# A hybrid mLSTM and latent attention step: two tiles' statistics ahead of the sample skip on VectorE, two inverse roots ahead of the gate product on GpSimd

## The chip, the cores and the metric

The kernel runs on one core of a Trainium2 chip. Its time is the device time of one execution in microseconds; the median of 3 runs is given. All arithmetic is float32. A core has a matrix engine (TensorE, PE in the profile), three engines for elementwise work (VectorE = DVE, ScalarE = ACT, GpSimd = POOL), an engine that here issues all transfers (SyncE = SP, its DMA queue SPq), and 16 DMA engines.

## What is computed

A prompt of 512 frames and 8 streams of 16 new frames (the sample rows) go through one mLSTM layer and one attention layer that share their weights. The change is in the mLSTM layer, which has 4 heads of width 512. Cut to what matters:

```
for each head:
    s   = (q k^T) * w_intra                       # within a chunk, causal
    num = w_inter * (C q) + s v
    den = w_inter * (n q) + sum(s)
    h   = num / max(|den|, exp(-m))
    C_new = decay * C + (v * w_upd)^T k           # 8 old states of 512 x 512 per head, and one new one
    n_new = decay * n + sum(w_upd * k)
hn = (h - mean(h)) * rsqrt(var(h) + eps) * outnorm_w     # per row and head
y  = (hn + skip * xc) * silu(z)
x  = x + y @ w_out
```

Then follow the shared latent keys and values, the attention layer and the output norms, which the change doesn't touch.

## The kernel before

The 640 rows are 5 tiles of 128: tiles 0 to 3 are the prompt, tile 4 (`NP`) holds the sample rows. Each engine has its own program, written out by hand in order, and the programs are tied by semaphores. No scheduler moves anything. An engine that waits holds up all that stands behind it in its program.

The four heads (numbered 0 to 3) run from about 310 to 570 us. In each, TensorE runs eight steps (`step(h, n)`: the products with one eighth of the old states, L1001, and their updates, L1016) mixed with the values of the prompt tiles (`prompt_values`, L1025), the transposition of normalised tiles (`turn`, L1034), and four quarters of the prompt's new state (`prompt_c`, L1049); then it starts the projections of the next head (`project_head`: L887, L900) and its scores.

A prompt tile goes round the engines like this: TensorE writes its values into PSUM and raises `pv_mm`; VectorE's `statistics(h, t)` (L2154 to L2173, seven small operations) raises `var_ready`; GpSimd's `inverse_root(h, t)` (L2617 to L2621) raises `pow_ready`; ScalarE's `normalise(h, t)` (L1611) empties the PSUM bank and raises `norm_done`; TensorE turns the tile. `prompt_c(h, 0)` writes into the bank of tile 2, so it waits for `norm_done` of that tile.

The sample rows of head h - 1 are finished in head h: VectorE adds the skip (`add_skip(h - 1, ...)`, L2201, four operations of 128x128; it raises `y_added`), and GpSimd multiplies by the gate (`gated(h - 1, ...)`, L2638; it waits for `y_added` and raises `y_ready`). GpSimd's `add_k(h, t)` (L2632) sums the weighted keys of the prompt tiles.

SyncE issues all transfers on one queue in a written order. Per step: the store of the updated state (L617, 1 MB) once VectorE's `update` (L2181) is done, then the load of a later state (L569, 1 MB) once the store of the step before has landed. Behind step 1 stands the load of the gate rows into `zh` (L624, 1.25 MB):

```
if n == 1:
    if h:
        sp.wait_ge(y_ready, 2 * h)
    sp.dma_start(zh, chunks(z_dram, h, slice(0, T))).then_inc(hz_in, 16)
```

The count 2h is reached by `gated(h - 1, slice(SEQ, T), 2)`, the last reader of the old `zh`. The load of the rows m (L602) comes next. The four quarters of the prompt's new state are copied out of PSUM by ScalarE's `keep_c(h, q)` (L1629, raises `pc_out`) into two buffers in turn, and stored (L592, 256 KB each: quarter 0 before step 4's store, 1 and 2 before step 5's, 3 before step 6's). So the copy of quarter 3 waits until the store of quarter 1 has landed:

```
if 2 * h + q // 2:
    act.wait_ge(cp_out[q % 2], 16 * (2 * h + q // 2))
```

`project_head(h + 1)` waits for `pc_out` of all four quarters of head h, and so does `first_out` (L720), the output projection behind head 3.

Of the kernel before, what the change touches and what calls it, by code (L numbers as in the profile page):

```python
# [155 lines left out]
def program(nc, i, o):  # L156

    with ExitStack() as ctx:
# [1666 lines left out]
        def _(dve):  # L1825
# [319 lines left out]
            def keep_sums(h):  # L2145
                dve.wait_ge(small_mm, 2 * h + 1)
                v.tensor_copy(den_s, small[:, 0:16]).then_inc(small_out, 1)
                dve.wait_ge(small_out, 2 * h + 1)

            def statistics(h, t):  # L2150
                src = pair_bank[t % 2] if t < NP else stream_h
                own, den = tiny[:, t], den_s[:, S_DEN + t:S_DEN + t + 1]
                dve.wait_ge(pv_mm, TT * h + t + 1)
                v.bn_stats(st6[:, t], src).then_inc(dve_own, c.up(dve_own))  # L2154
                if t == NP:
                    v.tensor_tensor(nqm, den_s[:, S_NQ:S_NQ + STREAMS], wq_mask[:, h], ALU.mult).then_inc(dve_own, c.up(dve_own))
                    dve.wait_ge(dve_own, c.all(dve_own))
                    v.reduce_sum(nq[:, 0:1], nqm, AX_X).then_inc(dve_own, c.up(dve_own))
                    dve.wait_ge(dve_own, c.all(dve_own))
                    v.tensor_tensor(nq[:, 1:2], nq[:, 0:1], den, ALU.add).then_inc(dve_own, c.up(dve_own))  # L2160
                    dve.wait_ge(dve_own, c.all(dve_own))
                    den = nq[:, 1:2]
                v.scalar_tensor_tensor(own[:, 1:2], den, -1.0, den, ALU.mult, ALU.max).then_inc(dve_own, c.up(dve_own))
                dve.wait_ge(dve_own, c.all(dve_own))
                v.bn_aggr(mv[:, t], st6[:, t]).then_inc(dve_own, c.up(dve_own))
                v.tensor_tensor(own[:, 1:2], own[:, 1:2], cols[:, 1, t, h:h + 1], ALU.max).then_inc(dve_own, c.up(dve_own))
                dve.wait_ge(dve_own, c.all(dve_own))
                v.reciprocal(own[:, 2:3], own[:, 1:2]).then_inc(dve_own, c.up(dve_own))
                dve.wait_ge(dve_own, c.all(dve_own))
                op = v.tensor_scalar(own[:, 4:5], mv[:, t, 1:2], own[:, 2:3], None, ALU.mult)  # L2170
                op.then_inc(dve_own, c.up(dve_own))
                dve.wait_ge(dve_own, c.all(dve_own))
                op = v.tensor_scalar(own[:, 3:4], own[:, 4:5], own[:, 2:3], EPS, ALU.mult, ALU.add)  # L2173
                op.then_inc(var_ready, 1)

            def update(h, n):
                s, par = STEPS * h + n, n // KH
                for g in range(4):
                    b = 2 * g + par
                    dve.wait_ge(upd_mm, 4 * s + g + 1)  # L2180
                    op = v.scalar_tensor_tensor(ct[s % CS][:, g, :], ct[s % CS][:, g, :], decb[:, h, b:b + 1],  # L2181
                                                bank[g][:, :], ALU.mult, ALU.add)
                    op.then_inc(upd_done, 1)
# [12 lines left out]
            def add_skip(h, part, tile):  # L2196
                dve.wait_ge(turn_out, TT * h + tile + 1)
                for q in range(KH):
                    n = h * KH + q
                    raised = y_added if q == KH - 1 else dve_own  # L2200
                    v.scalar_tensor_tensor(h_t[:, q, part], xc[:, n, part], vec[:, V_SK + n:V_SK + n + 1],  # L2201
                                           h_t[:, q, part], ALU.mult, ALU.add).then_inc(raised, c.up(raised))
# [14 lines left out]
            for h in range(HEADS):  # L2217
                keep_sums(h)
                statistics(h, 0)
                update(h, 0)  # L2220
                statistics(h, 1)
                update(h, 1)
                if h:
                    add_skip(h - 1, slice(SEQ, T), NP)
                statistics(h, 2)
                statistics(h, 3)
                update(h, 2)
                update(h, 3)
                update(h, 4)
                update(h, 5)  # L2230
                add_skip(h, slice(0, SEQ), NP - 1)
                new_n(h)
                update(h, 6)
                if h + 1 < HEADS:
                    head_front(h + 1)
                update(h, 7)
                if h + 1 < HEADS:
                    weighted_scores(h + 1, 0)
                statistics(h, NP)
                if h + 1 < HEADS:  # L2240
                    weighted_scores(h + 1, 1)
                    stream_queries(h + 1)
                    for t in range(2, TT):
                        weighted_scores(h + 1, t)
# [263 lines left out]
        def _(pool):  # L2508
# [105 lines left out]
            def inverse_root(h, t):  # L2614
                own = tiny[:, t]
                pool.wait_ge(var_ready, TT * h + t + 1)
                g.tensor_tensor(own[:, 4:5], own[:, 3:4], half_neg, ALU.pow).then_inc(pool_own, c.up(pool_own))  # L2617
                pool.wait_ge(pool_own, c.all(pool_own))
                g.tensor_tensor(own[:, 5:6], own[:, 4:5], own[:, 2:3], ALU.mult).then_inc(pool_own, c.up(pool_own))
                pool.wait_ge(pool_own, c.all(pool_own))  # L2620
                op = g.tensor_scalar(own[:, 6:7], mv[:, t, 0:1], own[:, 5:6], -1.0, ALU.mult, ALU.mult)  # L2621
                op.then_inc(pow_ready, 1)

            def add_k(h, t):
                if t == 1:
                    pool.wait_ge(kw_ready, 6 * (h + 1))
                    first = kh[:, :, 0, :]
                else:
                    pool.wait_ge(pool_own, c.all(pool_own))
                    first = kwsum  # L2630
                raised = kwsum_ready if t == NP - 1 else pool_own
                g.tensor_tensor(kwsum, first, kh[:, :, t, :], ALU.add).then_inc(raised, c.up(raised))  # L2632
# [21 lines left out]
            for h in range(HEADS):  # L2654
                sum_weights(h)
                inverse_root(h, 0)
                inverse_root(h, 1)
                if h:
                    gated(h - 1, slice(SEQ, T), 2)
                add_k(h, 1)  # L2660
                inverse_root(h, 2)
                add_k(h, 2)
                inverse_root(h, 3)
                add_k(h, 3)
                if h + 1 < HEADS:
                    head_basis(h + 1)
                gated(h, slice(0, SEQ), 1)
                inverse_root(h, NP)
# [241 lines left out]
```

## Time and profile before

| | us |
|---|---|
| median of 3 runs | 1042.89 (1042.45 to 1043.36) |
| the profiled execution's own time | 1039.92 |
| its span | 1038.1 |
| TensorE busy | 1010.7 |
| VectorE busy | 520.0 |
| GpSimd busy | 300.6 |
| ScalarE busy | 258.0 |

The granted clock of TensorE is full in all of the 40 slices. Busy time of an engine adds up its instructions; what is worth something to the time is where TensorE stands idle, and who ends that. A row of a timeline merges instructions of a kind that follow each other; in brackets stand the idle time before them and the instruction that ended it.

### The profile page before, as it was taken

The page shows a single profiled execution, that of the slowest core. Times are in us where ns is not written, and L with a number is a line of the kernel's source. Part 1 is how long each engine was busy: PE and PEld are TensorE (multiplying, and loading weights), DVE is VectorE, ACT ScalarE, POOL GpSimd, SP SyncE. Part 2 cuts the span into 40 slices and gives each one's busy share as a digit, 9 for nine tenths or more (in the row PEclk, how much of TensorE's full clock was granted, in tenths as well). Part 3 has the DMA queues.
Part 4 walks back from the last instruction along what each step waited for, and adds up shares of the span by engine and source line. Part 5 has one row for each costly group of instructions (what it writes and reads, how often), then busy time and mean ns, then how long its engine had stood idle before and what let it go on. Part 6 is the DMA issues. An engine that isn't in the chain of part 4 may idle for free.

```text
span 1038.1 us, 12026 instructions
## 1 busy us (share of the span) xinstructions
PE 1010.7 (97%) x4310; PEld 648.1 (62%) x4310; DVE 520.0 (50%) x1149; ACT 258.0 (25%) x541; POOL 300.6 (29%) x361
## 2 busy tenths in 40 slices
PE   7999999999989999999999999999999999999998
PEld 5777777777754453443535677777766666656655
DVE  6955444444466566685665522334244444344224
ACT  3212121212154242232421000011213323243221
POOL 3652525252313234142232053411440303010110
PEclk9999999999999999999999999999999999999999
DMA  7324232423275988979799432022210201213202
GB/s 271 98 80 158 97 113 105 157 91 111 112 286 191 399 329 345 370 303 392 300 350 340 154 107 71 32 81 104 93 63 1 84 17 68 73 47 128 79 27 102
DMA packets 44465, 164.21 MB, mean 158 GB/s; under 512 B 4916, under 2 KB 8248, under 8 KB 35456
## 3 DMA queue, kind: packets, MB, share of 16 engines
q1 hardware_dynamic: 44416, 163.56, 42.8%
q8 instruction: 30, 0.49, 0.2%
q14 instruction: 19, 0.16, 0.0%
HBM read 106.32 MB, written 57.23 MB: 158 GB/s over the span
## 4 chain that ended last, share of the span: by engine, by line
PE 85%; DVE 8%; ACT 2%; POOL 2%; DMA 1%; issue 1%; SPq 0%; DVEq 0%; POOLq 0%; ACTq 0%
PE work_a L825 11%; PE work_b L825 9%; PE work_a L720 7%; PE work_b L720 5%; PE work_b L1258 5%; PE work_a L1049 5%; PE bank L1133 5%; PE work_b L1342 4%; PE work_a L948 4%; PE bank L770 3%; PE bank L1016 2%; PE work_b L1133 2%; PE work_b L1001 2%; DVE arena L2181 2%; PE work_a L1328 2%; PE bank L1303 2%
## 5 line engine op out<-in xcount | busy, mean ns | idle before, releaser
L2181 DVE SCALAR_TENSOR_TENSOR arena<-arena,bank 128x512 f32<-128x512 f32 x128 | 87.1, 743 | 58.7 <-PE bank L1016 58.7
L1049 PE MATMUL work_a<-arena 128*128 128x512 f32 x128 | 64.1, 613 | 2.8 <-ACT arena L1611 2.8
L825 PE MATMUL work_a<-arena 128*128 128x320 f32 x224 | 64.9, 433 | 0.4 <-DVE arena L1948 0.4
L825 PE MATMUL work_a<-arena,ring 128*128 128x320 f32 x224 | 64.9, 432 | 0.0
L825 PE MATMUL work_b<-arena 128*128 128x320 f32 x224 | 62.8, 432 | 0.0
L720 PE MATMUL work_a<-arena,ring 128*128 128x320 f32 x192 | 54.2, 441 | 6.8 <-DMA ring<-in_stream 6.8
L825 PEld LDWEIGHTS work_b<-arena 128*128 128x128 f32 x224 | 42.6, 190 | 17.7
L720 PE MATMUL work_b<-arena,ring 128*128 128x320 f32 x192 | 52.8, 432 | 0.0
L2716 POOL COPY arena<-arena 32x640 f32<-32x640 f32 x20 | 16.9, 844 | 123.1 <-ACT arena L1726 116.9
L825 PEld LDWEIGHTS work_a<-arena 128*128 128x128 f32 x224 | 41.5, 190 | 16.1 <-issue 0.6
L825 PEld LDWEIGHTS work_a<-arena,ring 128*128 128x128 f32 x224 | 41.5, 190 | 15.5
L720 PEld LDWEIGHTS work_a<-arena,ring 128*128 128x128 f32 x192 | 37.2, 195 | 22.2 <-DMA ring<-in_stream 6.8
L2638 POOL TENSOR_TENSOR xc<-arena 128x2048 f32<-128x2048 f32 (+1 forms) x8 | 23.2, 2897 | 89.4 <-DVE arena L2201 89.4
L1493 ACT ACTIVATE arena<-arena 128x128 f32<-128x128 f32 x16 | 5.0, 314 | 168.0 <-DVE arena L1908 150.5
L770 PEld LDWEIGHTS bank<-arena 128*128 128x128 f32 x320 | 41.6, 190 | 7.0 <-ACT arena L1519 2.1
L720 PEld LDWEIGHTS work_b<-arena,ring 128*128 128x128 f32 x192 | 36.4, 190 | 15.0
L770 PE MATMUL bank<-arena 128*128 (+1 forms) x320 | 42.6, 280 | 1.1 <-ACT arena L1519 1.1
L1973 DVE SCALAR_TENSOR_TENSOR arena<-arena,vec 128x512 f32<-128x512 f32 x48 | 38.1, 795 | 5.0 <-ACT arena L1500 1.6
L948 PE MATMUL work_a<-xc,arena 128*128 128x128 f32 (+3 forms) x136 | 39.2, 431 | 0.7 <-ACT arena L1546 0.7
L1025 PE MATMUL work_a<-arena 128*128 128x512 f32 x80 | 38.1, 607 | 0.0
L1049 PEld LDWEIGHTS work_a<-arena 128*128 128x128 f32 x128 | 21.1, 190 | 26.5 <-issue 26.5
L1016 PE MATMUL bank<-arena 32*128 32x512 f32 x256 | 36.5, 640 | 0.0
(349 smaller groups left out, 1917.4 us busy)
## 6 DMA issues: line engine op xcount, KB each, us to landing
ring<-in_stream SPq DMA_DIRECT2D x66, 512.0 KB, 3.7
arena<-in_c SPq DMA_DIRECT2D x32, 1024.0 KB, 9.2
out_s_c<-arena SPq DMA_DIRECT2D x32, 1024.0 KB, 6.6
arena<-in_keys SPq DMA_DIRECT2D x8, 664.0 KB, 4.1
v_scratch<-arena SPq DMA_DIRECT2D x16, 320.0 KB, 4.4
k_scratch<-arena SPq DMA_DIRECT2D x16, 320.0 KB, 4.7
z_scratch<-arena SPq DMA_DIRECT2D x16, 320.0 KB, 4.2
arena<-k_scratch SPq DMA_DIRECT2D x4, 1280.0 KB, 12.6
```

Of the source, the lines that this page charges most:

```text
L720: done = mm(halves(buf)[:, a, :], lhs, rhs[:, a * HALF:(a + 1) * HALF], start=first, stop=last)
L770: last = mm(bank[2 * q + t // 3][:, at:at + VG], lhs, basis[:, q, n, :], start=True, stop=True)
L825: last = mm(quarter[q], weights[:, k, :], tokens_of[:, k, :], start=fresh and k == 0, stop=k == KH - 1, skip_group_check=True)
L948: last = mm(score_bank(h, t), k_t[:, q, q0:q0 + P], xc[:, h * KH + q, q0:q0 + WID[t]], start=q == 0, stop=q == KH - 1)
L1016: mm(bank[g][:, :], kz[h % 2][rows, par, q, :], v_s[h % 2][rows], start=True, stop=True, tile_position=(32 * g, 0)).then_inc(upd_mm, 1)
L1025: last = mm(pair_bank[t % 2], weights_of(s, t), vh[:, :, s, :], start=s == 0, stop=s == t)
L1049: last = mm(pair_bank[q % 2], kh[:, q, t, :], vh[:, :, t, :], start=t == 0, stop=t == NP - 1)
L1133: last = mm(dst[:, 0:HALF], weights[:, k, :], tokens_of[:, k, :], start=k == 0, stop=k == KD - 1)
L1258: last = mm(work[1][:, w * SEQ:(w + 1) * SEQ], out_weight(t, k), og[:, k, 0:SEQ], start=k == 0, stop=k == KD - 1)
L1342: last = mm(dst, weights[:, k, :], tokens_of[:, k, :], start=fresh and k == 0, stop=k == KH - 1, skip_group_check=True)
L1973: op = v.scalar_tensor_tensor(a0, xin[s][:, tap:tap + SEQ], w, a0, ALU.mult, ALU.add)
L2181: op = v.scalar_tensor_tensor(ct[s % CS][:, g, :], ct[s % CS][:, g, :], decb[:, h, b:b + 1], bank[g][:, :], ALU.mult, ALU.add)
```

## The change

In VectorE's program `statistics(h, 2)` and `statistics(h, 3)` go ahead of the skip of the preceding head's sample rows. In GpSimd's program `inverse_root(h, 2)` and `inverse_root(h, 3)` and two of the three `add_k` go ahead of the gate product of those rows, and `inverse_root(h, 3)` ahead of `add_k(h, 2)`.

```
@@ VectorE
                 update(h, 0)
                 statistics(h, 1)
                 update(h, 1)
+                statistics(h, 2)
+                statistics(h, 3)
                 if h:
                     add_skip(h - 1, slice(SEQ, T), NP)
-                statistics(h, 2)
-                statistics(h, 3)
                 update(h, 2)
@@ GpSimd
                 sum_weights(h)
                 inverse_root(h, 0)
                 inverse_root(h, 1)
+                add_k(h, 1)
+                inverse_root(h, 2)
+                inverse_root(h, 3)
+                add_k(h, 2)
                 if h:
                     gated(h - 1, slice(SEQ, T), 2)
-                add_k(h, 1)
-                inverse_root(h, 2)
-                add_k(h, 2)
-                inverse_root(h, 3)
                 add_k(h, 3)
```

VectorE's program in head 1, from the update of step 1 to that of step 2, before. L2154 opens one tile's statistics and L2173 closes them, L2201 is the skip, `work_a` the PSUM banks of the tiles.

```order
L2181 SCALAR_TENSOR_TENSOR arena<-arena,bank 128x512 x4
L2201 SCALAR_TENSOR_TENSOR arena<-xc,vec,arena 128x128 x4
L2154 BN_STATS arena<-work_a 128x6
L2163 SCALAR_TENSOR_TENSOR arena<-arena 128x1
L2165 BN_AGGR arena<-arena 128x2
L2166 TENSOR_TENSOR arena<-arena 128x1
L2168 RECIPROCAL arena<-arena 128x1
L2170 TENSOR_SCALAR arena<-arena 128x1
L2173 TENSOR_SCALAR arena<-arena 128x1
```

The same place now, from the opening of tile 3's statistics on (those of tile 2 stand ahead of it).

```order
L2154 BN_STATS arena<-work_a 128x6
L2163 SCALAR_TENSOR_TENSOR arena<-arena 128x1
L2165 BN_AGGR arena<-arena 128x2
L2166 TENSOR_TENSOR arena<-arena 128x1
L2168 RECIPROCAL arena<-arena 128x1
L2170 TENSOR_SCALAR arena<-arena 128x1
L2173 TENSOR_SCALAR arena<-arena 128x1
L2201 SCALAR_TENSOR_TENSOR arena<-xc,vec,arena 128x128 x4
L2181 SCALAR_TENSOR_TENSOR arena<-arena,bank 128x512 x16
```

The skip stands behind both tiles' statistics, and the four updates that follow stand directly behind the skip.

GpSimd's program at the same place, before: from the gate product (L2638) to the last `add_k` (L2632); L2617 opens an inverse root.

```order
L2638 TENSOR_TENSOR xc<-arena 128x4x128
L2632 TENSOR_TENSOR arena<-arena 128x512
L2617 TENSOR_TENSOR arena<-arena 128x1
L2619 TENSOR_TENSOR arena<-arena 128x1
L2621 TENSOR_SCALAR arena<-arena 128x1
L2632 TENSOR_TENSOR arena<-arena 128x512
L2617 TENSOR_TENSOR arena<-arena 128x1
L2619 TENSOR_TENSOR arena<-arena 128x1
L2621 TENSOR_SCALAR arena<-arena 128x1
L2632 TENSOR_TENSOR arena<-arena 128x512
```

And now.

```order
L2632 TENSOR_TENSOR arena<-arena 128x512
L2617 TENSOR_TENSOR arena<-arena 128x1
L2619 TENSOR_TENSOR arena<-arena 128x1
L2621 TENSOR_SCALAR arena<-arena 128x1
L2617 TENSOR_TENSOR arena<-arena 128x1
L2619 TENSOR_TENSOR arena<-arena 128x1
L2621 TENSOR_SCALAR arena<-arena 128x1
L2632 TENSOR_TENSOR arena<-arena 128x512
L2638 TENSOR_TENSOR xc<-arena 128x4x128
L2632 TENSOR_TENSOR arena<-arena 128x512
```

The gate product has gone behind two `add_k` and both inverse roots. The programs of TensorE, ScalarE and SyncE are the same as before.

## Rows read from the trace of the kernel before

**Rows 1.** The page, parts 1 and 2 (GB/s moved in 40 slices).
```profile
PE 1010.7 (97%) x4310; PEld 648.1 (62%) x4310; DVE 520.0 (50%) x1149; ACT 258.0 (25%) x541; POOL 300.6 (29%) x361
GB/s 271 98 80 158 97 113 105 157 91 111 112 286 191 399 329 345 370 303 392 300 350 340 154 107 71 32 81 104 93 63 1 84 17 68 73 47 128 79 27 102
```

**Rows 2.** Waits of TensorE and SyncE, 310 to 570: us, times, longest.
```profile
PE work_a L887 <- issue: 3.1, 3, 1.6
PE work_a L1049 <- ACT arena L1611: 2.8, 3, 0.9
SPq L624 <- POOL xc L2638: 4.6, 3, 1.5
```

**Rows 3.** Timeline of TensorE: start, us, line, operation, [idle before <- releaser].
```profile
365.48 1.13 PE L887 MATMUL work_a<-xc,arena 128*128 128x128 f32 x8 [1.28 <-issue]
...
395.97 3.60 PE L1025 MATMUL work_a<-arena 128*128 128x512 f32 x8
...
402.55 1.95 PE L1049 MATMUL work_a<-arena 128*128 128x512 f32 x4 [0.92 <-ACT arena L1611]
...
428.69 1.13 PE L887 MATMUL work_a<-xc,arena 128*128 128x128 f32 x8 [0.31 <-issue]
```

**Rows 4.** Timeline of ScalarE, end of heads 1 and 3.
```profile
428.00 0.60 ACT L1629 ACTIVATE arena<-work_a 128x512 f32<-128x512 f32 x1 [6.34 <-DMA out_p_c<-arena]
...
555.67 0.60 ACT L1629 ACTIVATE arena<-work_a 128x512 f32<-128x512 f32 x1 [6.34 <-DMA out_p_c<-arena]
```

**Rows 5.** Busy time in a stretch of head 1, clock, DMA share, GB/s.
```profile
393.00:428.00 35.00, 34.08 (x158) 14.03 (x158) 22.46 (x47) 8.49 (x23) 12.24 (x22) 1.00 1.01 383
```

**Rows 6.** Single issues (first and last start) and their time to landing.
```profile
L617 SPq DMA_DIRECT2D out_s_c<-arena x1: 343/343/343, 391.7 to 391.7; - x1
DMA to landing us min/median/max: 4.8/4.8/4.8
...
L592 SPq DMA_DIRECT2D out_p_c<-arena x1: 901/901/901, 418.5 to 418.5; - x1
DMA to landing us min/median/max: 9.4/9.4/9.4
...
L592 SPq DMA_DIRECT2D out_p_c<-arena x1: 332/332/332, 556.3 to 556.3; - x1
DMA to landing us min/median/max: 2.8/2.8/2.8
```

**Rows 7.** Timeline of VectorE, head 1.
```profile
386.12 0.70 DVE L2154 BATCH_NORM_STATS2 arena<-work_a 128x6 f32<-128x512 f32 x1 [0.86 <-PE work_a L1025]
...
387.62 0.21 DVE L2173 TENSOR_SCALAR arena<-arena 128x1 f32<-128x1 f32 x1
...
395.85 1.13 DVE L2201 SCALAR_TENSOR_TENSOR arena<-xc,vec,arena 128x128 f32<-128x128 f32 x4
...
397.51 0.90 DVE L2163 SCALAR_TENSOR_TENSOR arena<-arena 128x1 f32<-128x1 f32 x1
```

**Rows 8.** Timeline of GpSimd, head 1.
```profile
397.13 1.27 POOL L2638 TENSOR_TENSOR xc<-arena 128x512 f32<-128x512 f32 x1 [2.56 <-DVE arena L2201]
398.36 1.26 POOL L2632 TENSOR_TENSOR arena<-arena 128x512 f32<-128x512 f32 x1
400.42 0.55 POOL L2617 TENSOR_TENSOR arena<-arena 128x1 f32<-128x1 f32 x1 [0.80 <-DVE arena L2173]
...
401.33 0.26 POOL L2621 TENSOR_SCALAR arena<-arena 128x1 f32<-128x1 f32 x1
```

**Rows 9.** The loads of zh and their time to landing: heads 1 and 2, head 3.
```profile
L624 SPq DMA_DIRECT2D arena<-z_scratch x2: 379/379/379, 398.4 to 461.8; - x2
DMA to landing us min/median/max: 9.5/9.5/9.5
...
L624 SPq DMA_DIRECT2D arena<-z_scratch x1: 379/379/379, 526.3 to 526.3; - x1
DMA to landing us min/median/max: 10.8/10.8/10.8
```

More of the change, by code:

```diff
@@ L2222, in _ @@
                 update(h, 1)
+                statistics(h, 2)
+                statistics(h, 3)
                 if h:
                     add_skip(h - 1, slice(SEQ, T), NP)
-                statistics(h, 2)
-                statistics(h, 3)
                 update(h, 2)
@@ L2657, in _ @@
                 inverse_root(h, 1)
+                add_k(h, 1)
+                inverse_root(h, 2)
+                inverse_root(h, 3)
+                add_k(h, 2)
                 if h:
                     gated(h - 1, slice(SEQ, T), 2)
[L2660 to L2663, printed above, removed]
                 add_k(h, 3)
```

## The prediction, made before the changed kernel was run

> **What bounds the kernel now.** I read the page first: TensorE is busy for 97% of the span [rows 1], so a change elsewhere pays only where TensorE stands still. The list of TensorE's waits, cut to the four mLSTM heads (310 to 570 us), has two entries that matter here: 2.8 us in 3 waits of L1049 (the first matmul of `prompt_c`) for ScalarE's L1611 (`normalise`), and 3.1 us in 3 waits of L887 (the first matmul of `project_head`), which the profile puts down to "issue" [rows 2]. These two are one story.
>
> The first wait stands in heads 1 to 3, 0.92 us each time [rows 3]. What it waits for is `normalise(h, 2)`, behind `inverse_root(h, 2)` on GpSimd, behind `statistics(h, 2)` on VectorE, behind the skip of the sample rows of the head before.
>
> The second wait is named by the code and by ScalarE's timeline. `project_head(h + 1)` wants `pc_out` at 4 per head, which the copy L1629 of the fourth quarter raises. That copy waits 6.34 us for a DMA: the store of the second quarter, whose buffer it reuses. It starts at 428.00, takes 0.60, and L887 starts at 428.69, 0.09 us behind its end [rows 3, 4]. So from here to there TensorE is paced by a store's landing. Head 0 shows what that means: it has no skip ahead of its statistics and no wait at L1049, and still its L887 waits, 1.28 us, where head 1 waits 0.92 and then 0.31 [rows 3]. The sum is the same (1.28 against 1.23): time won at L1049 is taken back at L887.
>
> Why that store lands when it does is in the DMA rows. From 393 to 428 us of head 1 the DMA engines are busy without a gap (share 1.01) at 383 GB/s [rows 5]. The store of a 256 KB quarter lands 2.8 us after its issue where nothing is ahead of it, and 9.4 us after its issue at 418.5 [rows 6]: it stands in a queue, which all of SyncE's issues share.
>
> **The change, part by part.** Everything moved is in the head loop, and no instruction is added or taken away.
>
> VectorE, heads 1 to 3. `statistics(h, 2)` now starts where the skip started, at 395.85, and without the gate product beside it. Undisturbed, one takes 387.62 + 0.21 - 386.12 = 1.7 us. Before, the one for tile 2 ran beside L2638: its small L2163 alone took 0.90 us and ended together with GpSimd's product at 398.4 [rows 7, 8]. (The Trainium skill, "SBUF — State Buffer", section "SBUF: two separate sides", calls the pair of ports that VectorE and GpSimd share an exclusive lock, held for a whole instruction; this row behaves so, and no term below rests on it.) So its result is there at 395.85 + 1.7 = 397.6; before, GpSimd took it up at 400.42. GpSimd's three small operations, 1.2 us (400.42 to 401.33 + 0.26) [rows 8], and ScalarE's normalisation follow at once, and the wait of 0.92 goes. Alone that would be 3 x 0.92 = 2.8 us.
>
> The other side: the skip now stands behind `statistics(h, 3)`, which must wait for the values of tile 3. TensorE finishes these at 395.97 + 3.60 = 399.57 [rows 3]. Then: statistics to 401.4 (0.1 to start, 1.7), GpSimd's inverse root to 402.65 (0.1 to start, 1.2), `add_k` 1.26 to 403.9, and only then the gate product, 1.27 to 405.2. Before, it ended at 397.13 + 1.27 = 398.4 [rows 8]. It is 6.8 us later.
>
> Who waits for it: `gated` raises `y_ready`, on which SyncE waits before it issues the load of `zh`, and SyncE was already waiting there (4.6 us in 3 waits) [rows 2]: the load was issued at 398.4, as the product ended [rows 9]. Now it goes at 405.2. Queued behind it on SyncE: the load of the rows m (L602), the store and the load of step 2, and all that follows.
>
> What that costs: the z load used to be issued while the queue was full. Issued 6.8 us later it comes to an empty one. From two loose points, 2.8 us for 256 KB and 4.8 us for 1 MB [rows 6], a transfer costs 2.1 us fixed and 2.7 per MB, so its 1.25 MB land after 5.5 us. Head 1: 405.2 + 5.5 = 410.7, before 398.4 + 9.5 = 407.9, so 2.8 later. Head 2 has the same 9.5 [rows 9] and the same 2.8. Head 3: 526.3 + 6.8 + 5.5 = 538.6, before 526.3 + 10.8 = 537.1 [rows 9], so 1.5 later. Behind the z load the engines have no gap in which to make it good (share 1.01), so the store that paces L887 lands later by as much, and by way of L1629 TensorE starts the next head (after head 3, the output projection: L1629 at 555.67 is held by the same store, 6.34 us [rows 4]) later by as much. The 0.92 us saved shows up inside that longer wait: L887 of head 1 would be reached at 427.5 and start at 431.5, a wait of 4.0 us instead of 0.31. The next head starts with everything shifted, the loads of k and v too, so the terms add.
>
> Sum: 2.8 + 2.8 + 1.5 = 7.1 us. Bounds of one head's term: below, -0.92 (the transfers don't matter, and the wait is saved); above, 6.8 (all of the z load's delay arrives). I take the queue's account, since the row nearest to it, the store that lands 9.4 us after its issue, is a queue's.
>
> At nothing I cost: head 0's change on GpSimd (its product order only, with no gate product and no wait behind it); `update(h, 2)`, which starts some 0.6 us later behind the skip, hidden by the 4 us that TensorE now waits at L887; `add_k` and `head_basis`, whose results are wanted 15 us later.
>
> Own time of the profiled execution: 1039.9 us with a span of 1038.1; it becomes 1047.0. It stands 3.0 us under the median of the runs, 1042.9, which becomes 1050.0.
>
> **Rivals.**
>
> Partly made good. The stretch ran at 383 GB/s, and the best slice of the page at 399 with the same kinds of transfer [rows 1, 5]. If a fuller queue ran at 399, the 25 us behind the gap would give back 25 x (1 - 383/399) = 1.0 us a head: 7.1 - 3.0 = 4.1, so 1047.0. For it: single rows of the queue differ that much (z after 9.5 and 10.8 us). Against: the share is 1.01, there is no idle time to fill.
>
> Faster. The small store isn't held by what stands ahead of it, the z load's lateness finds room, and L1049's wait is won: the store's issue moves 0.92 us earlier with `update(h, 4)`, and L887 with it. -2.8, so 1040.1. Against it: head 0's 1.28, and 9.4 against 2.8 us for the same store. The Trainium skill has a rule on its side ("DMA: Bandwidth & Descriptors", section "Queues, rings and completion order"): completion is not first in, first out per issuing engine. The same section has each engine take descriptors in ring order, and the 9.4 us agree with that half.
>
> No change. The z load's delay is harmless, but the pacing store stands where it stood: 0.92 moves from L1049 to L887. 1042.9. For it: heads 0 and 1. Against: the z load is ahead of that store in the same queue.
>
> Slower still. The z load, the m rows, a store and a load are now issued in one burst, so the old state for step 5 lands some 3 us later too, and TensorE stops for it inside the head or the store slips once more. About 1 us a head more: 10.1, so 1053. It decides once TensorE shows a wait at L1001 for DMA.
>
> **How the numbers follow.** Full delay 0.58 (1050.0, its own range 1048 to 1052), partly made good 0.20, slower still 0.06, no change 0.08, faster 0.08. What a measurement can tell from no change is about 0.2%, 2.1 us. Faster 0.08; the same 0.09 (no change, and a sliver of the second case); slower 0.83. The range runs from 1045 to 1053: it leaves out the two cases below and little above.
>
> **What would show it.** Right: no wait at L1049 for L1611; L2638 of the sample rows ends near 405.2 in head 1 and L624 is issued just behind it; a hole of 2 to 3 us in the DMA share between 403 and 406; L592's second store lands near 430.7; the waits at L887 grow from 3.1 us to some 11 (1.3, then 0.3 + 0.9 + 2.8 = 4.0, then 1.6 + 0.9 + 2.8 = 5.3), and a further 2 to 3 us appear at L720 after head 3. Wrong: a DMA share that stays full there, or L887's waits unchanged while L624 is late. Then the store doesn't stand behind the z load, and the time would be at or under that of before.

## The result, and the profile after

The changed kernel takes 1053.69 us (median of 6 runs, 1050.8 to 1055.94); beside it the kernel before takes 1042.9 (1040.61 to 1043.36). The ratio is 1.0102, interval 1.0082 to 1.0121: slower, as predicted, but past the predicted 1050.0 and 0.7 us outside the range. The profiled execution took 1050.91 us with a span of 1049.1, against 1039.92 and 1038.1 before: 11.0 us more.

The page's parts 1 and 2 for the kernel after (busy time of each engine; TensorE's granted clock in 40 slices, in tenths):

```profile
PE 1017.4 (97%) x4310; PEld 652.9 (62%) x4310; DVE 512.8 (49%) x1149; ACT 258.0 (25%) x541; POOL 301.4 (29%) x361
PEclk9999999999999999899999999999999999999999
```

TensorE executes the same 4310 products but is busy 6.7 us longer than in [rows 1]. Waits alone lengthen the span, not the busy time, so this is the first sign that something beside waits is at work. One slice has an 8 in the clock row, where before all were full.

The waits of TensorE and then of SyncE's queue, 310 to 580 us (total, times, longest):

```profile
PE work_a L887 <- issue: 7.6, 3, 3.6
PE work_a L720 <- ACT arena L1629: 2.4, 1, 2.4
PE work_b L1001 <- DMA arena<-in_c: 1.1, 1, 1.1
```

```profile
SPq L624 <- POOL xc L2638: 25.2, 3, 8.4
```

Against [rows 2], L1049's 2.8 us are gone, L887's 3.1 have become 7.6, and 2.4 at L720 and 1.1 at L1001 are new. SyncE waits 25.2 us instead of 4.6 for the gate product: 6.9 a head, where 6.8 was predicted.

Head 1 on VectorE and on GpSimd, timelines (start, us, line, operation, [idle before <- releaser]). The profiled execution is 2.26 us late by then (most of it outside the change, below), so 2.26 has to be taken off for a comparison with rows of before.

```profile
401.86 0.70 DVE L2154 BATCH_NORM_STATS2 arena<-work_a 128x6 f32<-128x512 f32 x1 [2.04 <-PE work_a L1025]
...
403.50 1.13 DVE L2201 SCALAR_TENSOR_TENSOR arena<-xc,vec,arena 128x128 f32<-128x128 f32 x4
```

```profile
405.00 1.28 POOL L2632 TENSOR_TENSOR arena<-arena 128x512 f32<-128x512 f32 x1
406.24 1.28 POOL L2638 TENSOR_TENSOR xc<-arena 128x512 f32<-128x512 f32 x1
```

The load of `zh` in head 1 (first and last start; time to landing):

```profile
L624 SPq DMA_DIRECT2D arena<-z_scratch x1: 379/379/379, 407.5 to 407.5; - x1
...
DMA to landing us min/median/max: 6.3/6.3/6.3
```

The product ends and the load goes at 407.5, or 405.2 without the shift: the predicted time to a tenth. It lands after 6.3 us (5.5 predicted), where the load of [rows 9] took 9.5 in its full queue.

Stretches of the kernel after (from:to, length, busy us of PE, PEld, DVE, ACT, POOL, then granted clock, DMA share, GB/s):

```profile
316.00:320.00 4.00, 4.00 (x16) 3.29 (x15) 3.22 (x13) 2.72 (x10) 0.00 (x0) 0.57 0.91 332
...
398.00:407.00 9.00, 9.00 (x39) 3.73 (x38) 6.68 (x23) 2.64 (x8) 4.22 (x9) 1.00 0.84 345
407.00:410.00 3.00, 3.00 (x20) 0.65 (x18) 0.26 (x1) 1.60 (x4) 3.00 (x6) 1.00 0.41 88
410.00:433.00 23.00, 19.68 (x100) 8.41 (x96) 14.24 (x24) 3.95 (x11) 6.13 (x6) 0.98 1.02 409
433.00:436.00 3.00, 2.77 (x10) 2.54 (x11) 0.00 (x0) 0.73 (x2) 0.00 (x0) 0.50 1.02 406
436.00:440.00 4.00, 4.00 (x10) 2.59 (x9) 1.01 (x3) 0.88 (x2) 0.00 (x0) 0.61 1.02 368
440.00:444.00 4.00, 4.00 (x23) 1.53 (x22) 2.63 (x8) 2.85 (x9) 0.00 (x0) 1.00 0.99 398
```

The DMA column shows the hole, 88 GB/s from 407 to 410, and behind it 409 GB/s where [rows 5] had 383 over the whole stretch. The clock column shows what the prediction had no term for: 0.50 and 0.61 right after the wait at L887, that is 1.2 GHz (the lower of the clock's two levels; the other is 2.4) for some 6 of these 7 us.

ScalarE's copies of quarters 2 and 3, then TensorE:

```profile
427.07 0.60 ACT L1629 ACTIVATE arena<-work_a 128x512 f32<-128x512 f32 x1 [7.37 <-DMA out_p_c<-arena]
432.54 0.60 ACT L1629 ACTIVATE arena<-work_a 128x512 f32<-128x512 f32 x1 [4.87 <-DMA out_p_c<-arena]
```

```profile
403.82 1.98 PE L1049 MATMUL work_a<-arena 128*128 128x512 f32 x4
...
433.23 2.04 PE L887 MATMUL work_a<-xc,arena 128*128 128x128 f32 x8 [3.56 <-issue]
...
437.20 2.20 PE L900 MATMUL bank<-xc,arena 128*128 128x320 f32 x4
...
440.31 1.24 PE L900 MATMUL bank<-xc,arena 128*128 128x320 f32 x4
...
489.70 1.06 PE L1001 MATMUL work_b<-arena 128*32 128x512 f32 x8 [1.09 <-DMA arena<-in_c]
...
501.58 1.13 PE L887 MATMUL work_a<-xc,arena 128*128 128x128 f32 x8 [2.37 <-issue]
...
565.93 3.84 PE L720 MATMUL work_a<-xc,ring 128*128 128x320 f32 x8 [2.42 <-ACT arena L1629]
...
571.77 2.42 PE L720 MATMUL work_a<-xc,ring 128*128 128x320 f32 x8
```

L1049 starts with no wait, and L887 starts 0.09 us behind the copy's end, as in [rows 3, 4]. Its eight products take 2.04 us instead of 1.13, and the four of L900 2.20 instead of 1.24. The output projection does the same: 3.84 behind the wait, 2.42 for eight products of the same form a little later. The wait of 2.37 at 501.58 is followed by products at full clock.

**The 11.0 us of the profiled execution**, by the shift of the same instruction against before: 2.26 at L887 of head 0, of which 1.6 are there ahead of 316 us (nearly all since the first 12 us of the kernel), 0.3 come in from 316 to 324, and 0.35 are a longer wait at that L887 (1.63 instead of 1.28); 2.28 from there to L887 of head 1; 2.68 more while the clock is low behind it; 1.02 in head 2, with the wait at L1001 inside; 1.36 in head 3; 1.42 of low clock behind that. Transfers: 2.28 + 1.02 + 1.36 = 4.7, predicted 7.1. Low clock behind waits: 2.68 + 1.42 = 4.1, predicted nothing. Together they are 8.8 of the 11.0; the 2.26 in front of them can't be put down to the change. The stretch of low clock at 316 to 320, which the trace of before has not, delays TensorE by 1.5 us, but its waits for GpSimd's L2651 just behind are then 1.3 us shorter (0.5 instead of 1.8).

### The profile page after: what moved, and what is told of

It is laid out like the page before. It is cut to its first block, busy times and chain, and to the rows that moved or that the text cites. A ratio compares the mean times of both kernels' runs of the same rounds, so it can differ in the third digit from the quotient of the medians.

```text
span 1049.1 us, 12026 instructions
## 1 busy us (share of the span) xinstructions
PE 1017.4 (97%) x4310; PEld 652.9 (62%) x4310; DVE 512.8 (49%) x1149; ACT 258.0 (25%) x541; POOL 301.4 (29%) x361
## 4 chain that ended last, share of the span: by engine, by line
PE 61%; DMA 3%; DVE 2%; POOL 2%; issue 1%; ACT 1%; SPq 0%; POOLq 0%; ACTq 0%
PE work_a L720 6%; PE work_b L1258 5%; PE work_b L720 5%; PE bank L1133 5%; PE work_b L1342 4%; PE work_a L1049 4%; PE work_a L1025 3%; PE work_a L948 3%; PE bank L1016 3%; PE work_b L1001 2%; PE work_b L1133 2%; PE work_a L1328 2%; PE bank L1303 2%; PE work_a L1288 1%; PE bank L1455 1%; PE work_a L1133 1%
## 5 line engine op out<-in xcount | busy, mean ns | idle before, releaser
L1049 PE MATMUL work_a<-arena 128*128 128x512 f32 x128 | 64.2, 613 | 0.0
L720 PE MATMUL work_a<-arena,ring 128*128 128x320 f32 x192 | 55.4, 448 | 7.2 <-DMA ring<-in_stream 7.2
L720 PE MATMUL work_b<-arena,ring 128*128 128x320 f32 x192 | 52.8, 432 | 0.0
L720 PEld LDWEIGHTS work_a<-arena,ring 128*128 128x128 f32 x192 | 37.9, 198 | 23.1 <-DMA ring<-in_stream 7.2
L825 PEld LDWEIGHTS work_a<-arena 128*128 128x128 f32 x224 | 41.5, 190 | 16.1 <-issue 0.6
L720 PEld LDWEIGHTS work_b<-arena,ring 128*128 128x128 f32 x192 | 36.4, 190 | 15.0
L2638 POOL TENSOR_TENSOR xc<-arena 128x2048 f32<-128x2048 f32 (+1 forms) x8 | 23.2, 2898 | 74.8 <-DVE arena L2201 74.8
L2617 POOL TENSOR_TENSOR arena<-arena 128x1 f32<-128x1 f32 x20 | 11.1, 554 | 106.7 <-DVE arena L2173 106.7
L1016 PE MATMUL bank<-arena 32*128 32x512 f32 x256 | 36.5, 640 | 0.0
```

The lines of the kernel that those rows point to most:

```text
L720: done = mm(halves(buf)[:, a, :], lhs, rhs[:, a * HALF:(a + 1) * HALF], start=first, stop=last)
L825: last = mm(quarter[q], weights[:, k, :], tokens_of[:, k, :], start=fresh and k == 0, stop=k == KH - 1, skip_group_check=True)
L1016: mm(bank[g][:, :], kz[h % 2][rows, par, q, :], v_s[h % 2][rows], start=True, stop=True, tile_position=(32 * g, 0)).then_inc(upd_mm, 1)
L1049: last = mm(pair_bank[q % 2], kh[:, q, t, :], vh[:, :, t, :], start=t == 0, stop=t == NP - 1)
```

## The experiments

Each ran beside the kernel before on the same chip; ratios are to it, with their 95% interval. The code cuts are shortened. The medians of the kernel before were 1041.71 (e1 to e4), 1041.54 (e5 to e8), 1043.57 (e9 to e12) and 1042.69 (e13 to e16). Theory: the late `zh` load delays the transfers behind it. Rivals: the moved instructions themselves cost the time, on VectorE or GpSimd; or the transfers are innocent and TensorE's clock does it alone.

### Is it the load of zh?

e1: the kernel before, whose SyncE alone is held until the last of the head's three `add_k` is done.

```
 if h:
     sp.wait_ge(y_ready, 2 * h)
+    sp.wait_ge(kwsum_ready, h + 1)
 sp.dma_start(zh, ...)
```

> The kernel before, with nothing moved on VectorE or GpSimd; only SyncE's load of the gate rows zh (L624) in heads 1 to 3 also waits for the last of the head's add_k, which the trace of before has ending at 405.2 us in head 1, the moment at which the changed kernel issued that load. Theory (the late load behind which all other transfers of the head queue is the loss): slower by 7 to 11 us, the three waits of 0.92 us at L1049 stay, the waits at L887 grow to at least 7 us in total, and TensorE's granted clock falls in some stretch behind the longest of them. Rival (the loss comes from the moved arithmetic, by the update of step 2 that starts later behind the skip): within 1 us of before.

1049.6 us (1046.19 to 1051.6), ratio 1.0071 (1.0047 to 1.0094). TensorE's waits, its start of head 1, and two stretches of it:

```profile
PE work_a L888 <- issue: 7.2, 3, 3.0
PE work_a L1050 <- ACT arena L1612: 2.7, 3, 0.9
PE work_a L721 <- ACT arena L1630: 1.5, 1, 1.5
```

```profile
367.56 1.57 PE L888 MATMUL work_a<-xc,arena 128*128 128x128 f32 x8 [1.79 <-issue]
```

```profile
368.00:372.00 4.00, 4.00 (x14) 2.98 (x13) 1.33 (x3) 1.03 (x2) 0.45 (x1) 0.57 0.93 342
500.00:504.00 4.00, 3.58 (x13) 2.83 (x14) 1.03 (x3) 0.99 (x3) 0.15 (x1) 0.65 1.02 418
```

No instruction of VectorE or GpSimd is moved, and most of the loss is there, with the grown waits at L887 and L720 one line further down (the added line shifts the numbers). L1050 keeps its 2.7 us, so saving them isn't what the next head pays with. The low clock at 368 stands behind a wait of only 1.79 us.

e12: GpSimd's order as changed, VectorE's as before.

```
 inverse_root(h, 1)
-if h: gated(h - 1, slice(SEQ, T), 2)
 add_k(h, 1); inverse_root(h, 2)
-add_k(h, 2); inverse_root(h, 3)
+inverse_root(h, 3); add_k(h, 2)
+if h: gated(h - 1, slice(SEQ, T), 2)
```

> Half of the change: GpSimd's program as changed, VectorE's as before. The statistics of tile 2 stand behind the skip but have no gate product beside them, so L1049's wait should go, and the gate product ends near 405 us as in the changed kernel. Theory (the late load of zh is the loss, whatever VectorE does): 7 to 12 us slower than before. Rival (VectorE's order makes the loss): within 2 us of before.

1050.84 us (1050.13 to 1051.81), 1.0080 (1.0066 to 1.0094). The gate product and the second of its two long waits:

```profile
405.82 1.28 POOL L2638 TENSOR_TENSOR xc<-arena 128x512 f32<-128x512 f32 x1
```

```profile
500.50 2.04 PE L887 MATMUL work_a<-xc,arena 128*128 128x128 f32 x8 [3.04 <-issue]
```

L1049's wait goes here too, although the skip still stands ahead of the statistics. In the trace of before, the statistics of tile 2 ran beside the gate product and an `add_k` on GpSimd and took 3.4 us (396.90 to 400.33); here, with nothing large beside them, they take 1.7. GpSimd's order carries most of the change by itself. What separates the 7.3 us of e12 and the 7.9 of e1 from the 10 to 10.8 of the whole change is not shown; VectorE's order alone was not run.

e2 and e3: four buffers for the copied-out quarters instead of two, on the kernel before and on the changed one. The copy of quarter 3 then waits for a store of the head before, long landed.

```
-cps = [take(HD) for _ in range(2)]
+cps = [take(HD) for _ in range(4)]
 ...
-    act.wait_ge(cp_out[q % 2], 16 * (2 * h + q // 2))
-nc.scalar.activation(cps[q % 2], pair_bank[q % 2], ACT.Copy)
+    act.wait_ge(cp_out[q], cp_before[q] + 16 * h)
+nc.scalar.activation(cps[q], pair_bank[q % 2], ACT.Copy)
```

> The kernel before, with four buffers instead of two between ScalarE's copy of a quarter of the prompt's new state (L1629) and its store (L592), so no copy waits for a store of the same head. Theory (a store's landing paces TensorE at L887): the 3.1 us of waits at L887 go and the kernel is about 3 us faster (1040). Rival (the wait at L887, which the profile calls issue, is TensorE's own): L887's waits and the time stay, within 1 us.

> The changed kernel with the same four buffers. Theory: the late load of zh can no longer reach TensorE by way of the store, so most of the loss goes: L887's waits under 1 us, L1049's gone, the time between 1038 and 1045; what is left is waits for old states (L1001) or for the keys, which stand behind the late load in the queue. Rival (the change costs by something else than the pacing store): it stays 8 us or more above the kernel before with four buffers.

e2: 1038.86 us, 0.9977 (0.9962 to 0.9992); no wait at L887 is left. e3: 1043.24, 1.0008 (0.9993 to 1.0022). Against e2, which has the same buffers, the change costs 4.4 us: with the pacing store out of the way, more than half of its 10.8 are gone, not all. The two longest waits of e3:

```profile
454.17 1.14 PE L1018 MATMUL bank<-arena 32*128 32x512 f32 x8 [2.77 <-ACT arena L1623]
486.20 1.06 PE L1003 MATMUL work_b<-arena 128*32 128x512 f32 x8 [1.85 <-DMA arena<-in_c]
```

The late queue now comes through at the next points, the keys of the next head (L1018) and the old state (L1003).

e8: of the two tiles only tile 2 goes ahead, on both engines, and no `add_k`.

> Half of the change: on VectorE only tile 2's statistics go ahead of the skip, on GpSimd only its inverse root goes ahead of the gate product. The gate product then ends near 400.2 us in head 1 instead of 398.4 or 405.2, so the load of zh is issued 1.8 us later than before, while the queue is still full. Theory (only the hole in the queue costs; the wait won at L1049 comes back at L887): L1049's wait is gone, L887's waits grow by about as much, the time within 1.5 us of before. Rival (earlier statistics help by themselves): 2 to 3 us faster. Rival (any delay of the load of zh costs its own length): 3 us or more slower.

1042.54 us, 1.0014 (0.9999 to 1.0030). The load goes at 401.2, or 400.2 without the 0.96 us by which this trace is late there: 1.8 us later than before instead of 6.8, and it costs nothing that can be told from no change. L1049's wait is gone, and 0.74 us at L1034 stand in its place.

### Is it the clock?

e4: the changed kernel with 24 products, thrown away, that TensorE does while it would stand at L887. e5 is the same with 10, at L887 and at L720; e11 has e5's edit on the kernel before, as a control.

```
+pe.wait_ge(pc_out, KH * h - 1)      # the third copy is done
+for _ in range(FILL):   # FILL = 24 in e4, 10 in e5 and e11
+    mm(pair_bank[0][:, 0:P], ones_f[:], ones_f[:], ...)
 pe.wait_ge(pc_out, KH * h)
```

> The changed kernel; ahead of L887, once the third copy L1629 is done, TensorE runs 24 products of 128x128 into a bank that is free there, some 3 us of work that is thrown away. No transfer and no wait is changed. Theory (behind the 3.6 us wait of head 1 the clock fell to about 0.55 for some 6 us, which cost 2.7 us there and 1.4 us behind head 3, as much as the waits themselves): with the wait filled the granted clock stays at 1.00 from 430 to 442 us and the kernel is 2 to 4 us faster than the changed one; the wait before head 3's successor isn't filled and may still cost its 1.4 us. Rival (the clock's fall has another cause than the wait): the clock falls as before and the time doesn't change or grows by the filler.

> As the filled wait, mended: 24 products took 5.6 us, where the wait was 3.6 us and less, so TensorE reached L887 late. Now 10 of them (2.3 us), ahead of L887 and ahead of L720 behind head 3, in the changed kernel. Theory (the clock's fall behind the grown waits is a part of the loss that the prediction left out, some 3 to 4 us of the 11): the granted clock stays at 1.00 behind all four waits, the mean clock of the runs rises from 0.992 to 0.995 or more, and the time is 2 to 5 us under the changed kernel's 1053.7. Rival (the waits do not draw the clock down; it falls as often by itself): the mean clock stays near 0.992 and the time within 1 us.

> Control for the short fill: the kernel before with the same 10 thrown-away products ahead of L887 and of the L720 behind head 3. Its waits there are 0.1 to 1.6 us, so the 2.3 us of products overrun them by some 1 to 2 us each. Theory (the fill helps the changed kernel by keeping the clock up behind long waits, not by anything else): no gain here, between 0 and 6 us slower than before, the mean clock as before. Rival (the fill helps in any kernel): faster than before.

e4: 1057.93 us, 1.0149 (1.0124 to 1.0174), a miss: the fill took 5.62 us, overran the wait, and cost more than it saved. e5: 1047.03, 1.0052 (1.0035 to 1.0070), mean clock 0.997 to 1.0, where the changed kernel's runs have 0.990 to 0.994. e11: 1047.53, 1.0051 (1.0034 to 1.0067): on the kernel before, whose waits are shorter than the fill, the same products cost 4 us. They help only where TensorE would have stood for long.

e13 and e14 put the changed kernel and e5's version on one chip.

> The changed kernel once more, on the same chip as the next. Theory (waits behind the late store 4 to 5 us, the clock's fall behind them 4 to 6 us): 9 to 12 us slower than before, mean clock 0.990 to 0.994. Rival (the first measurement was a slow chip's): less than 7 us slower.

> The changed kernel with the short fill, on the same chip. Theory: 4 to 7 us faster than the changed kernel, mean clock 0.997 or more. Rival (the fill gained nothing, the chips differ): within 2 us of it.

e13: 1052.7 us (1046.41 to 1056.75), 1.0109 (1.0091 to 1.0127). e14: 1046.64, 1.0050 (1.0035 to 1.0065). Ten idle products per wait take 6.1 us off, an estimated 5.1 of them by the mean clocks of the runs (0.993 and 0.998). e13's single runs go with their mean granted clock: the fastest, 1046.41, has 0.998, the slowest, 1056.75, 0.989. The 0.009 between them is 9.4 us of missing full clock, of 10.3 measured. e13's profiled execution is its fastest; two of its waits, and the stretches behind them:

```profile
430.69 1.13 PE L887 MATMUL work_a<-xc,arena 128*128 128x128 f32 x8 [3.47 <-issue]
...
496.66 1.59 PE L887 MATMUL work_a<-xc,arena 128*128 128x128 f32 x8 [4.03 <-issue]
```

```profile
430.00:436.00 6.00, 5.31 (x24) 3.85 (x24) 2.14 (x5) 2.50 (x5) 0.00 (x0) 1.00 1.02 399
...
496.00:500.00 4.00, 3.34 (x12) 2.76 (x13) 0.49 (x1) 1.15 (x2) 0.00 (x0) 0.65 1.01 414
```

So the same length of wait does not always bring the fall: 3.47 here without it, 3.04 in e12 with it. And this trace shows the change nearly without the clock's share: L887 +6.0, L720 +2.6, L1049 -2.8, 5.8 us in all. The rest goes with the clock: over the runs, its mean is 0.993 in e13 and 0.997 in the kernel before beside it, an estimated 0.004 x 1048 = 4.2 us, and 5.8 + 4.2 are the 10.0 measured. In e14 the fill and what is left of the wait:

```profile
427.93 2.50 PE L906 MATMUL work_a<-ones_f 128*128 128x128 f32 x20
431.45 1.16 PE L887 MATMUL work_a<-xc,arena 128*128 128x128 f32 x8 [1.02 <-ACT arena L1636]
```

e15 and e16 take the transfers out. Both start from the best version (e10, below), where TensorE has no such wait. ScalarE repeats the copy of quarter 3 eight times, so TensorE stands some 3.4 us ahead of each projection with no transfer late; e16 fills 2.9 us of it with 12 products.

```
+for _ in range(8 if q == KH - 1 else 0):   # each waits for the one before
+    nc.scalar.activation(cps[q], pair_bank[q % 2], ACT.Copy)
 nc.scalar.activation(cps[q], pair_bank[q % 2], ACT.Copy).then_inc(pc_out, 1)
```

> The idle slot with four buffers (1036, no wait at L887), where ScalarE now repeats the copy of quarter 3 of each head 8 times before it reports it. TensorE so stands still some 3 to 4 us ahead of L887 and of the L720 behind head 3, while no transfer is late but that quarter's store. Theory (a standstill of that length draws the clock down by itself): the four standstills cost their length, 12 to 16 us, and 3 to 10 us more in stretches of low clock; mean clock 0.993 or less. Rival (the clock falls only with the changed transfers): their length alone, mean clock 0.996 or more.

> The same, with 12 thrown-away products of TensorE (2.8 us) inside each standstill. No wait is shorter by it. Theory: faster than without them by 3 to 10 us, mean clock 0.997 or more. Rival: as long as without them, or longer.

e15: 1060.0 us (1055.97 to 1061.75), 1.0168 (1.0147 to 1.0189). e16: 1048.44 (1047.16 to 1050.75), 1.0061 (1.0046 to 1.0077). Two of e15's four standstills, and a stretch behind the second; then the same place in e16:

```profile
369.18 1.13 PE L889 MATMUL work_a<-xc,arena 128*128 128x128 f32 x8 [3.36 <-issue]
...
436.17 2.05 PE L889 MATMUL work_a<-xc,arena 128*128 128x128 f32 x8 [3.36 <-issue]
```

```profile
436.00:440.00 4.00, 3.83 (x12) 3.22 (x13) 0.49 (x1) 0.67 (x2) 0.00 (x0) 0.50 0.84 291
```

```profile
432.03 2.94 PE L908 MATMUL work_a<-ones_f 128*128 128x128 f32 x24
435.42 1.16 PE L889 MATMUL work_a<-xc,arena 128*128 128x128 f32 x8 [0.45 <-ACT arena L1641]
```

```profile
436.00:440.00 4.00, 4.00 (x20) 2.97 (x19) 1.48 (x3) 1.62 (x4) 0.00 (x0) 1.00 1.00 317
```

In both the projection starts right behind the held-back copy; only what TensorE did until then differs, and the time differs by 11.6 us over four standstills, 2.9 each. That isolates the clock: the transfers are not late, and TensorE could not have begun earlier. By mean clock it comes to the same: 0.986 in e15 and 0.997 in e16 are an estimated 11.5 us apart. And e16 stands 12.1 us above e10 by their ratios, close to the 4 x 3.4 = 13.4 us that the standstills last, so with the fill they cost about their length and no more. (Behind the first standstill of e15 the clock fell only 1.4 us after the start of the products, where behind the second it had fallen 0.8 us before it: the eight products run at full speed, the ones after them don't.)

The Trainium skill ("TensorE: Matmul & The Clock Gate", section "HAM oscillation — how this bites in real kernels") describes a kernel that pays the clock's fall anew at each wait for a transfer. The rows here agree that a standstill of TensorE can be paid twice (2.04 us for products of 1.13 behind 3.56 us of wait); they also show one of 3.47 us with full clock behind it.

### Can the load be moved, or the wait be won otherwise?

e6 and e7 move the `zh` load behind the stores of quarters 1 and 2, on the changed kernel and on the one before, so that it stands behind the pacing store.

```
-if n == 1: (wait for y_ready, load zh)
 store_prompt_c(h, 1); store_prompt_c(h, 2)
+if n == (5 if h + 1 < HEADS else 2): (wait for y_ready, load zh)
```

> The changed kernel; SyncE issues the load of zh behind the stores of quarters 1 and 2 (step 5) in heads 0 to 2, and ahead of step 2's store in head 3. The gate product of the prompt rows needs it only after step 5. Theory (the late load harms only by standing ahead of the store that paces L887 and by holding SyncE up): no wait at L1049, waits at L887 under 1.5 us in total, 1036 to 1042. Rival (the hole in the transfers costs wherever the load stands, since the engines are full for the rest of the head): above 1047.

> The kernel before, with the load of zh moved in the same way. Theory: 1.25 MB less stand ahead of the pacing store, so L887's 3.1 us of waits go, L1049's 2.8 us stay: 1039 to 1041. Against the changed kernel with the same move it shows what the earlier statistics are worth by themselves: 2.8 us. Rival (the pacing store isn't held by the load of zh): L887's waits and the time as before.

e6: 1047.78 us, 1.0059 (1.0036 to 1.0082), a miss: 1036 to 1042 were expected. L887 waits 0.6 in all, as the theory wants, but the gate product of head 0's prompt rows is now late and holds up VectorE. VectorE, GpSimd, and TensorE's L900, which waits for VectorE's L2041 just behind:

```profile
368.00 4.62 DVE L2118 TENSOR_TENSOR arena<-arena 128x256 f32<-128x256 f32 x1
```

```profile
367.84 4.50 POOL L2638 TENSOR_TENSOR xc<-arena 128x2048 f32<-128x2048 f32 x1 [21.91 <-DMA arena<-z_scratch]
```

```profile
373.07 1.44 PE L900 MATMUL work_b<-xc,arena 128*128 128x320 f32 x2 [4.13 <-DVE arena L2041]
```

L2118 takes 0.42 us with nothing beside it (at 436.96 and 499.41 of this trace). Here it starts 0.16 us behind GpSimd's product and ends 0.28 us behind its end, which fits the exclusive lock, held for a whole instruction, that the Trainium skill ("SBUF — State Buffer", section "SBUF: two separate sides") describes for the ports that VectorE and GpSimd share. Behind the 4.13 us the clock fell too: 0.51 from 374 to 378.

e7: 1048.27 us (1041.38 to 1054.15), 1.0071 (1.0041 to 1.0101), a miss: 1039 to 1041 were expected. Its profiled execution is its fastest and shows L887 at 2.0 and L1016 at 1.4 us, too little for the median; the three runs of 1053 us and more have a mean clock of 0.991 to 0.993, and none of these was profiled. Why they fall so often there stays open.

e9 keeps the load early and wins L1049's wait: the skip goes into VectorE's idle time between the statistics and the update of step 0, the gate product behind the first inverse root. e10 adds e2's four buffers.

```
 statistics(h, 0)
+if h: add_skip(h - 1, slice(SEQ, T), NP)
 update(h, 0); statistics(h, 1); update(h, 1)
-if h: add_skip(h - 1, slice(SEQ, T), NP)
```

> The kernel before, with the preceding head's skip put between statistics(h, 0) and update(h, 0), where VectorE stands idle for 1.1 us waiting for TensorE (387.83 to 388.96 in head 1), and the gate product behind the first inverse root. The statistics of tiles 2 and 3 are then free of the skip, and the load of zh is issued no later than before. Theory (a store's landing paces TensorE at L887): L1049's waits of 0.92 go, L887's grow by as much, the time within 1.5 us of before. Rival (removing L1049's wait is worth its 2.8 us once the load isn't late): 2 to 3 us faster.

> The same with four buffers for the quarters of the new state, so that no copy waits for a store. Both waits are gone, 2.8 us at L1049 and 3.1 at L887. Theory: about 6 us faster than before, some 3 us faster than the four buffers alone. Rival (something else, old states or keys, is hardly earlier, and takes over): as fast as the four buffers alone.

e9: 1041.28 us, 0.9983 (0.9972 to 0.9994). e10: 1035.92 (1034.77 to 1039.43), 0.9945 (0.9927 to 0.9963), the fastest of all. Their waits:

```profile
PE work_a L887 <- issue: 3.5, 3, 1.7
PE work_a L720 <- ACT arena L1629: 1.6, 1, 1.6
```

```profile
PE work_a L722 <- POOL xc L2640: 0.6, 1, 0.6
```

In e9 (first fence) L1049's 2.8 us are won, and 2.0 of them stand at L887 and L720 again: time won inside the head is handed back at its end while the store paces it, as the equal sums of 1.28 and 1.23 in the prediction said. The median is lower than that leaves: e9 is 1.8 to 2.3 us faster than before, past the 1.5 of its theory and near its rival. In e10 nothing hands time back, and it is some 3.3 us faster than e2 (ratios 0.9945 and 0.9977).

## Where the prediction was right, and where it failed

**Who paces the head.** Right. The store of quarter 1, by way of L1629, releases L887: 0.09 us apart in both traces, and e2 removes the wait by removing that dependence.

**The zh load goes 6.8 us later.** Right: 25.2 against 4.6 us of SyncE's wait, 6.9 a head. e1 loses 7.9 us by that delay with nothing moved on VectorE or GpSimd, and e12 7.3 with VectorE's order as before.

**The delay comes through at 2.8, 2.8 and 1.5 us, 7.1 in all.** The mechanism was right, the size too large: 4.7 us in the profile, 5.8 by the waits of e13, and waits of 7.6 us in all at L887 where 11 were forecast. In head 1 the load landed at 413.8, or 411.6 without the shift, 3.7 later than before. The 23 us behind the hole ran at 409 instead of 383 GB/s, which gives back 23 x (1 - 383/409) = 1.5 us: 2.2 come through. That is the rival "partly made good", argued against with "there is no idle time to fill"; a DMA share of 1.01 isn't a full rate. It is an estimate: the trace of before itself moved 406 GB/s from 398 to 408 us and 375 from 411 to 428.

SyncE's own waits give the same figure another way. Before (404 to 420 us), then after (404 to 424), total, times and longest:

```profile
SPq L617 <- DVE arena L2181: 14.9, 3, 6.0
```

```profile
SPq L569 <- DMA out_s_c<-arena: 7.6, 2, 4.5
```

Ahead of the pacing store stands the load of step 4, which waits for the store of step 3 to land. That store landed at 416.6 before (issued at 411.5, 5.1 to landing) and at 422.5 after (412.8, 9.7), 3.7 later once the shift is off: the whole delay of the z load. But before, SyncE didn't need it until 418.0, since VectorE's update released step 4 only then. These 1.4 us of slack were not in the sum either, and 3.7 - 1.4 is 2.3. The pacing store, issued right behind at 422.9 (2.1 later), landed 9.5 us after its issue, 9.4 before. Whether the higher rate or the slack is what gave the time back, no run separates.

**L1049's wait goes and shows up inside the longer wait.** Right (L887 of head 1: 3.56, of which 0.9 were L1049's), and e9 shows the same with the load not late.

**Slower still, by a late old state.** True in one head only: 1.1 us of wait at L1001, inside head 2's 1.02.

**What has no term: the clock.** The failed step is a silent one. "TensorE starts the next head later by as much" costed a wait at its own length. Behind waits of 2.4 to 4.1 us TensorE's clock often stood at 1.2 GHz for several us, and its products took nearly twice as long. It is worth 4.1 us in the profiled execution, 6.1 on one chip (e13 against e14), 11.6 where it was made on purpose (e15 against e16). 5.8 of transfers and 4.2 of clock make the 10.0 us of e13; the profile that belongs to the 10.8 us measured first has 4.7 and 4.1. The predicted 7.1 was a transfer term too large by 1.3 to 2.4 us, with the clock missing; that it came within 4 us of the result is in part luck, since the two errors go against each other. The profile of before shows no fall in the heads, and its waits at L887 are 1.6 us at most; but it is one execution at full clock, and the kernel before falls too: in the round of e1 its seven fastest runs (1039.58 to 1040.85) have mean clocks of 0.998 to 1.0, and those at 0.996 take 1042.4 to 1045.95. The 3.0 us by which the profile stood under the median were a hint of the missing term.

Not settled: why a standstill brings the fall at one time and not at another, why e7 loses what it loses, and why the clock is low at about 316 to 320 us, with no wait of TensorE just before, in most profiles (e2 has it at 321 to 328), but not in those of before, e7, e13 and e14.

## What to carry to other kernels

Look for the dependence that ends each iteration before costing a reorder inside it: time won inside is handed back there, while a transfer delayed in a full, ordered queue is passed on to it. Price a TensorE wait that grows to some 3 us at more than its length, with the clock's fall as a term and a range of its own; read the granted clock in short stretches behind each long wait, since 40 slices hide it, and in the other runs too, since one profile may show none of it. A DMA share of 1.0 says that the engines have work, not that they can't move it faster.

## What the runs showed of the hardware that was not expected

- The length of a standstill does not decide alone whether the clock falls: 3.47 us without a fall (e13), 3.04 (e12) and even 1.79 (e1) with one. A difference of 0.009 in mean clock goes with 10 us of run time (e13).
- Products on constants, thrown away inside the waits, pay for themselves where these are long (-6.1 us over waits of 1.7 to 4.0, -11.6 over four of 3.4) and cost about 4 us where the waits are shorter than the fill (e11).
- With the DMA share at 1.01 and 1.02, the rate was 383 GB/s in one stretch (before, 393 to 428) and 409 in the other (after, 410 to 433).
- A VectorE operation of 0.42 us took 4.62 beside a GpSimd product of 4.50 (e6), and the statistics of a tile 3.4 us instead of 1.7 beside two of 1.3 (before, e12).
